# The second mixer as one phase: gates, heads, head norm and output product share one stream of weight tiles, with pairs of heads overlapped

## The reference, cut to what matters

```python
def _mlstm_mix(x, w_in, conv_w, conv_b, b_i, b_f, hn_w, w_out):
    p = x @ w_in                                   # 1024 -> q,k (64 per head), v,o (128 per head), 16 gates
    qk = silu(causal_dwconv(p[..., :1024], conv_w, conv_b))
    v, o, gi, gf = ...                             # the other columns of p
    log_i = softcap(gi + b_i);  log_f = log_sigmoid(softcap(gf + b_f))
    # per head, F = cumsum(log_f), m_t = the running stabiliser:
    # w[t, s]  = exp(F_t - F_s + log_i_s - m_t) * (q_t . k_s) / 8      for s <= t
    # num = w @ v;  den = max(|sum_s w|, exp(-m_t));  h = num / den
    h = h * rsqrt(mean(h * h, -1) + 1e-6) * hn_w   # over the 128 values of a head
    return (h * sigmoid(o)) @ w_out

x = x + g1 * _mlstm_mix(rms(x) * (1 + sc1) + sh1, ...)
```

## Time and profile before

| what | value |
|---|---|
| median of 3 runs | 4840.05 us (4831.29 to 4841.23) |
| the profiled execution | 4829.72 us, span 4828.0 us |
| second mixer, from the end of the norm ahead of it to its last instruction | 3925.0 to 4382.4 us of the span, 457.4 us |
| of that: gates, heads, head norm with the wait for the output weights, output product | 37.3, 313.7, 58.0, 48.4 us |
| TensorE busy in the span | 4274.8 us (89%) |
| mean granted TensorE clock | 0.942 of full speed |

### The profile page before, as it was taken

One profiled execution on the slowest core, in us unless ns is written; L12 is line 12 of the kernel. 1 busy time (PEld: TensorE's weight loads), 2 busy tenths in 40 slices (PEclk: granted clock), 3 DMA queues, 4 the chain that ended last, 5 costly groups with the idle time before them and its releaser, 6 DMA issues. The chain is left out here.

```text
span 4828.0 us, 65725 instructions
## 1 busy us (share of the span) xinstructions
PE 4274.8 (89%) x25274; PEld 3197.5 (66%) x25274; DVE 2312.4 (48%) x4304; ACT 1472.0 (30%) x1985; POOL 1312.9 (27%) x534
## 2 busy tenths in 40 slices
PE   5999879959999999999999779899789868847988
PEld 3777633338888888788888533788668735426866
DVE  6877756547886888322222331556332122353211
ACT  2555510023334444322222101343234111122421
POOL 2322200024443333345454200111234300003432
PEclk9999989989999999999999889899899988868999
DMA  4222177614334555556556221000122211101221
GB/s 148 91 87 93 61 282 285 230 49 131 126 129 159 178 180 178 187 181 195 184 187 190 79 64 51 12 3 3 36 91 96 100 44 52 43 18 65 96 107 53
DMA packets 222607, 548.79 MB, mean 114 GB/s; under 512 B 32272, under 2 KB 100496, under 8 KB 212320
## 3 DMA queue, kind: packets, MB, share of 16 engines
q1 hardware_dynamic: 205472, 546.27, 33.3%
q10 hardware_dynamic: 16960, 0.13, 0.2%
HBM read 470.68 MB, written 75.66 MB: 113 GB/s over the span
## 5 line engine op out<-in xcount | busy, mean ns | idle before, releaser
L1510 POOL TENSOR_TENSOR peer_wl<-peer_wf,peer_wh 128x1024 fp32r<-128x1024 f32 x272 | 717.1, 2637 | 971.1 <-ACT peer_wh L1523 971.1
L1597 PE MATMUL peer_y<-peer_xh,peer_wh 128*128 128x512 f32 x1152 | 455.9, 396 | 30.2 <-DVE peer_xl L1669 30.2
L1523 ACT ACTIVATE peer_wh<-peer_wf 128x1024 fp32r<-128x1024 f32 x272 | 286.2, 1052 | 547.7 <-PE peer_y L1599 513.4
L1599 PE MATMUL peer_y<-peer_xh,peer_wl 128*128 128x512 f32 x1152 | 449.6, 390 | 0.0
L1598 PE MATMUL peer_y<-peer_xl,peer_wh 128*128 128x512 f32 x1152 | 449.5, 390 | 0.0
L1628 PE MATMUL peer_y<-peer_twh,peer_wh 128*128 128x512 f32 x1024 | 405.7, 396 | 11.7 <-DVE peer_twl L1737 11.7
L1629 PE MATMUL peer_y<-peer_twl,peer_wh 128*128 128x512 f32 x1024 | 405.5, 396 | 0.0
L1630 PE MATMUL peer_y<-peer_twh,peer_wl 128*128 128x512 f32 x1024 | 405.5, 396 | 0.0
L1737 DVE TENSOR_TENSOR peer_twl<-peer_gout,peer_twh 128x512 fp32r<-128x512 f32 x128 | 90.8, 710 | 503.6 <-ACT peer_twh L1584 503.6
L1809 PE MATMUL up_acc<-up_xh,up_wh 128*128 128x512 f32 x704 | 276.6, 393 | 47.2 <-DVE up_xl L1859 47.2
L1794 POOL TENSOR_TENSOR up_wl<-up_wf,up_wh 128x1024 fp32r<-128x1024 f32 x88 | 211.3, 2401 | 343.2 <-ACT up_wh L1823 343.2
(11 more groups left out here) (499 smaller groups left out, 8587.4 us busy)
## 6 DMA issues: line engine op xcount, KB each, us to landing
mix_aw<-in_w_ada SPq DMA_DIRECT2D x32, 2048.0 KB, 9.4
peer_wf<-in_u SPq DMA_DIRECT2D x128, 512.0 KB, 3.6
peer_wf<-in_v SPq DMA_DIRECT2D x128, 512.0 KB, 3.7
up_wf<-in_w_gu SPq DMA_DIRECT2D x88, 512.0 KB, 3.2
br_wf<-in_w_in SPq DMA_DIRECT2D x64, 512.0 KB, 3.6
acts<-peer_aout SPq DMA_DIRECT2D x128, 256.0 KB, 2.0
gates<-peer_gout SPq DMA_DIRECT2D x16, 2048.0 KB, 7.3
peer_gout<-gates SPq DMA_DIRECT2D x32, 1024.0 KB, 7.1
```

The costliest lines, as they stand in the source:

```text
L1510: nc.gpsimd.tensor_tensor(wl[:, t % SLOTS], wf[:, t % 2], wh[:, t % SLOTS], ALU.subtract).then_inc(w_low, 1)
L1523: nc.scalar.activation(wh[:, t % SLOTS], wf[:, t % 2], ACT.Copy).then_inc(w_high, 1)
L1597: nc.tensor.matmul(out, wh[:, slot, k], xh[:, k], start=(k == 0), stop=False)
L1599: last = nc.tensor.matmul(out, wl[:, slot, k], xh[:, k], start=False, stop=(k == KT - 1))
```

## The change

One function replaces the four parts. It has one list of 32 weight tiles, 24 for the inputs and 8 for the output, which SP loads, ACT and POOL split and PE consumes in the same order, two buffers deep. All large products are made of three matmuls (lines 2686 to 2688 of the new file, and 2698 to 2700 for the output).

The rounds run i = 0 to 4. In round i PE makes the six products of pair i, and between them the small products of pair i-1 (scores, numerator, denominator, sums of squares), and in front the spread of the normalising factors of pair i-2. The value tiles are now made like the others, and turned by four transposes (`vt`). The denominator is made as a column of sums per token instead of a broadcast matrix: ten matmuls with one column each, whose stationary operand is the weights themselves. Its division and the norm are then done together on tiles of 128x4: DVE's reciprocals (2983, 2994) and ACT's square root (2865). ACT expands the factor to 128x512 (2870), and PE turns it by a product with the identity (2756). The last round has no new products. There PE makes the first six of eight parts of two output tiles (`HELD`) ahead of the last head's norm.

Of the stabilisers only m is stored. The eight broadcast rows are loaded once, into `C.H`, which nobody reads by then. The residual is updated straight from PSUM by one DVE instruction per tile (3060) instead of two.

```diff
-        mlstm_gates_phase(nc, io, C, ngc)
-        mlstm_phase(nc, io, C, h, gate, ngc)
-        norm_phase(nc, C, "mlnorm", h, h, KT, 1, P, EPS_RMS, weight=lambda t: C.v("hn_w", t), times=gate)
-        split_residual_phase(nc, C, "mlout", io["w_ml_out"], KT, 2, 2, 1.0, src=h)
+    mlstm_phase(nc, io, C)
...
             @block.sync
             def _(sp):
+                sp.dma_start(wg[:], io["w_ml_gates"]).then_inc(gates_loaded, 16)
+                for tile, (kind, n) in enumerate(W):
+                    if tile >= 2:
+                        sp.wait_ge(w_low, tile - 1)
+                    sp.dma_start(wf[:, tile % 2], source(kind, n)).then_inc(loaded[tile % 2], 16)
+                    if tile == 3:
+                        sp.wait_ge(rows_ready, 2)
+                        sp.dma_start(io["stabilisers"][0], m).then_inc(m_stored, 16)
+                        sp.wait_ge(m_stored, 16)
+                        for h in range(2 * PAIRS):
+                            sp.dma_start(C.H[:, h], io["stabilisers"][0, h:h + 1].broadcast_to([P, S])
+                                         ).then_inc(rows_loaded, 16)
...
             @block.tensor
...
+                for i in range(PAIRS + 1):
+                    p, cur = i - 1, i < PAIRS
+                    if cur:
+                        project("q", i)
+                    if p >= 0:
+                        scores(2 * p)
+                    if cur:
+                        project("k", i)
+                    if p >= 0:
+                        scores(2 * p + 1)
+                    if p >= 1:
+                        spread(2 * p - 2)
+                        spread(2 * p - 1)
+                    if cur:
+                        project("v", 2 * i)
...
+                    if cur:
+                        project("g", 2 * i)
+                        turn_v(2 * i + 1)
+                    else:
+                        output(0, 0, HELD)
+                        output(1, 0, HELD)
...
             @block.scalar
...
+                def w_highs(tile):
+                    if tile >= len(W):
+                        return
+                    act.wait_ge(loaded[tile % 2], 16 * (tile // 2 + 1))
+                    if tile >= SLOTS:
+                        act.wait_ge(rounds, R.index[W[tile - SLOTS]] + 1)
+                    nc.scalar.activation(wh[:, tile % SLOTS], wf[:, tile % 2], ACT.Copy).then_inc(w_high, 1)
...
+                def keep_numerator(h):
+                    if h >= 2:
+                        act.wait_ge(o_low, h - 1)
+                    keep("n", h, num[:, h % 2])
+                    act.wait_ge(kept_s, R.place["n", h])
+                    nc.scalar.activation(sq[:, h % 2], num[:, h % 2], ACT.Square).then_inc(squared, 1)
...
             @block.vector
...
+                for i in range(PAIRS + 1):
+                    p, cur = i - 1, i < PAIRS
+                    if p >= 0:
+                        weights(2 * p)
+                        weights(2 * p + 1)
+                    if p >= 1:
+                        output(2 * p - 2)
+                        output(2 * p - 1)
+                    if cur:
+                        conv("q", i)
+                        conv("k", i)
+                    if p >= 1:
+                        output_low(2 * p - 2)
+                        output_low(2 * p - 1)
...
+                        decays(2 * i)
+                        decays(2 * i + 1)
+                    if p >= 0:
+                        combine(2 * p)
+                        combine(2 * p + 1)
+                        variance(2 * p)
+                        variance(2 * p + 1)
+                        invert(2 * p)
+                        invert(2 * p + 1)
```

More of the change, by code:

```diff
@@ L2517, in _ @@
                 output(last_pair)
[L2520 to L2533 removed]
+ML_PAIRS = 4
@@ L2545, in _, with result @@
             def _(pe):
[L2546 to L2552 removed]
+                stream = [0]
+                def result(name, n):
+                    pe.wait_ge(kept_s if R.who[name, n] == "s" else kept_v, R.place[name, n])
@@ new lines, in output @@
+                def output(n, first, end):
+                    out = begin("y", n) if first == 0 else of("y", n)
+                    pe.wait_ge(w_low, ML_TILES + n + 1)
+                    s = (ML_TILES + n) % SLOTS
+                    for kk in range(first, end):
+                        pe.wait_ge(o_low, kk + 1)
+                        nc.tensor.matmul(out, wh[:, s, kk], oh[:, kk], start=(kk == 0), stop=False)
+                        nc.tensor.matmul(out, wh[:, s, kk], ol[:, kk], start=False, stop=False)
+                        last = nc.tensor.matmul(out, wl[:, s, kk], oh[:, kk], start=False, stop=(kk == KT - 1))
+                    return last
@@ new lines, in spread @@
+                def spread(h):
+                    pe.wait_ge(f_rows, h + 1)
+                    out = begin("f", h)
+                    for tb in range(TB):
+                        at_b = slice(tb * P, (tb + 1) * P)
+                        last = nc.tensor.matmul(out[:, at_b], frow[:, h % 2, at_b], C.ident[:], start=True, stop=True)
+                    last.then_inc(rounds, 1)
+                pe.wait_ge(gates_loaded, 16)
+                for n, name in enumerate(("gi", "gf")):
+                    product(nc, begin(name, 0)[0:8], wg[:, :, 8 * n:8 * n + 8], C.H, KT).then_inc(rounds, 1)
@@ L2570, in _ @@
+                output_high(2 * LAST)
+                output_high(2 * LAST + 1)
+                for tile in range(ML_TILES + SLOTS, len(W)):
+                    w_highs(tile)
             @block.vector
@@ L2572, in _ @@
                 link = Chain(dve, chain_s)
[L2573 to L2580 removed]
+                tt, ts, stt = nc.vector.tensor_tensor, nc.vector.tensor_scalar, nc.vector.scalar_tensor_tensor
@@ L2752, in second_block @@
+                for h in (2 * LAST, 2 * LAST + 1):
+                    output(h)
+                    output_low(h)
+                for n in range(KT):
+                    x = C.X[:, n]
+                    kept(stt(out=x, in0=read("y", n), scalar=C.mod[:, COL + n:COL + n + 1], in1=x, op0=ALU.mult,
+                             op1=ALU.add), "y", n)
 def second_block(nc, io, C):
```

546 lines of the change are left out of this document (351 added, 195 removed).

## The result

The changed kernel takes 4673.62 us (median of 4 runs, 4669.78 to 4678.82); the kernel before took 4840.64 beside it (4 runs, 4831.29 to 4842.41). The ratio is 0.9659, with a 95% interval from 0.9642 to 0.9677. The forecast was 4678, range 4655 to 4706.

A forecast was written before the change was run, and what follows sets the result against it. The mixer was bound by engine-to-engine chains with barriers, afterwards by PE's own work. Gates, rounds and end made it 156.8 us shorter: 4672.9 from the profiled execution, 4683.3 off the median; forecast the middle, 4678, range 4655 to 4706.

The forecast's parts named there:

- The likeliest case: Whole program: PE's own work bounds the rounds, no stall within one; forecast 4678 us, chance 0.62.
- PE's work: A full round: six products at 5.63 us, denominators 2.3 per head (4.3 at the lower clock), together 52.2.
- The link that I had called the tightest: Next round's first weight tile: ready 49 us after the round's start, wanted by PE at 52.
- The fifth tile: Round 0: tile load waits behind the store of `m` and eight row loads; 6 us charged, bounds 0 and 13.
- DVE beside POOL: Each round: six meetings with POOL passes slow DVE by 1.8 us each, making DVE 34; it still fits.
- the signs that I had named for a right prediction: Mixer near 300 us, PE over 92% busy, rounds about 52, few PE waits at fifth tile and end, longer convolution steps.
- The end: After the fourth round, a chain through ACT, DVE and PE to the last eviction: 83.3 us, bounds 70 and 95.
- The middle between the two sums: Whole program: 4678, between 4672.9 (from the profiled execution) and 4683.3 (off the median of the runs).
- Stalls in every round: Rival: two PE stalls per round in three rounds add 33 us, 4711; one short stall each, 4690; chance 0.22.
- Better than the sum: Rival: row loads hide and the clock recovers sooner in the end, taking off 7.5 and some 8: 4662; chance 0.13.
- The clock at its lower level throughout: Rival: many small matmuls keep PE at its lower level, 216 us lost against 157 gained: 4894; chance 0.01.
- No overlap: Rival: each round is a serial pass, others' 35 us behind PE's 52; three rounds add 105, 4783; chance 0.02.

The follow-up runs named there:

- rows_late: Changed kernel with the store of `m` and the eight row loads issued behind the sixth tile's load instead of the fourth's: 4670.74 us, ratio 0.9649.
- dve_twice: Changed kernel with convolutions and decay weights computed twice on DVE, same result: 4679.98 us, ratio 0.9674.
- two_pass: Changed kernel without the pass of `wh` against `xl` in the 24 input products, 192 matmuls fewer: 4644.72 us, ratio 0.9610.
- tail: rows_late with the last round reordered: sums of squares, three eighths of output tile 0, spreads, then the rest so tile 0 ends first: 4667.31 us, ratio 0.9643.
- tail_wide: tail with 128 columns of ones in place of one in the matmuls of denominators and sums of squares: 4662.98 us, ratio 0.9630.
- four_pass: Changed kernel with a product of the two low halves added to each of 24 input tiles, 192 matmuls more: 4717.31 us, ratio 0.9756.
- ctrl: The changed kernel once more, nothing altered: 4673.45 us, ratio 0.9659.
- products_first: Changed kernel with a round's six products in a row, then all small matmuls of the pair before: 4679.86 us, ratio 0.9668.
- sums_first: Changed kernel with the last sums of squares ahead of the held output product and the spreads between its two tiles: 4670.21 us, ratio 0.9647.
- both: Changed kernel with the edits of rows_late and sums_first together: 4668.48 us, ratio 0.9647.
- plain_f32: Changed kernel with one float32 product of the high halves in place of the three passes of each input product: 4708.32 us, ratio 0.9734.
- two_pass_wide: two_pass with 128 columns of ones in place of one in the denominator matmuls: 4640.08 us, ratio 0.9584.

## Why the prediction was right

The likeliest case came true: PE bound in the rounds, one wait in round 0, a chain in the end. Its terms against the profile, in the order of the sum:

| step | forecast | measured |
|---|---|---|
| gates' load and product | 19.1 | 18.9 |
| round 0 with the fifth tile | 43.3 | 42.3 |
| of which that wait | 6 | 5.4 |
| rounds 1, 2, 3 | 50.4, 52.2, 52.2 | 49.5, 51.2, 51.3 |
| end | 83.3 | 78.6 |
| mixer | 300.5 | 291.8 |

**PE's work.** The products took 5.5 us each and the denominators 2.15 from start to start, against 5.63 and 2.3. I read my prices in `branches_phase` and in the pairs before; these small excesses make the 1 us a round. The choice of 2.3 and not 4.3 for the denominators was right, but my ground (they stand between products) covers only half of what the experiments show: their own price is 2.15 in all the profiles, and it is the product behind them that can run at the lower level.

**Slack.** The link that I had called the tightest, the next round's first tile, came out as told: ready 47.8 after the start of round 2 where I had 49, and wanted at 51.2 where I had 52. (The low half's pass ran from 4092.88 to 4095.28, the product began at 4098.68, the round before at 4047.43.)

**The fifth tile.** The store of `m` came where the sum had put it: forecast 3957.2, in a phase that in this execution began 11.8 later, so 3969.0.

```profile
3969.28 0.35 SPq L2647 DMA_DIRECT2D stabilisers<-ml_e  x1
3970.77 3.67 SPq L2650 DMA_DIRECT2D H<-stabilisers  x8
3974.48 22.23 SPq L2644 DMA_DIRECT2D ml_wf<-in_w_ml  x5
...
3981.23 1.06 ACT L2825 ACTIVATE ml_wh<-ml_wf 128x1024 fp32r<-128x1024 f32 x1 [8.10 <-DMA ml_wf<-in_w_ml]
...
3984.86 0.76 PE L2686 MATMUL ml_bank<-ml_xh,ml_wh 128*128 128x512 f32 x1 [5.37 <-POOL ml_wl L2660]
```

rows_late showed the cause. That the wait came out so near the 6 that I charged has luck in it. The terms that I named (2 for the store, 5 for the eight issues, 3.3 for the load) end at 3967.5, and I wrote 3970 without a term for the rest; in this execution that is 3979.3 and 3981.8. Measured, the store and the issues took less (5.2 from 3969.28 to 3974.48), and the load, beside the eight row loads, took 6.7 where I had 3.3: ACT's high half could start at 3981.23.

**DVE beside POOL.** Here a size was off. I charged 1.8 us for each of six meetings, 34 us of DVE a round; it was 23.5. No convolution step was slowed in the full rounds: eighteen of them, 752 ns each; at most the last of a group was still running when POOL's pass began. In rounds 2 and 3 POOL's passes hold up one group of masks and one of low halves:

```profile
4056.82 2.40 POOL L2660 TENSOR_TENSOR ml_wl<-ml_wf,ml_wh 128x1024 fp32r<-128x1024 f32 x1 [5.97 <-ACT ml_wh L2825]
4057.57 2.39 DVE L2963 TENSOR_TENSOR ml_e<-ml_e,keep 128x128 f32<-128x128 f32 x4
...
4072.65 2.70 POOL L2660 TENSOR_TENSOR ml_wl<-ml_wf,ml_wh 128x1024 fp32r<-128x1024 f32 x1 [7.40 <-ACT ml_wh L2825]
4073.05 3.44 DVE L3006 TENSOR_TENSOR ml_ol<-ml_num,ml_oh 128x512 fp32r<-128x512 f32 x2
```

The masks took 2.39 against 0.90 elsewhere, the low halves 3.44 against 1.47: two meetings, 1.5 and 2.0 lost. The price per meeting was about right and the count wrong. It did not matter, as dve_twice shows. Of the signs that I had named for a right prediction two failed: the convolution steps did not get longer, and the end had five waits of PE where I had named two or three (3.30, 1.43, 1.44, 1.06 and 1.14 us).

**The end.** My chain had the right links in the right order, and each was forecast 6 to 19% late. From the start of the last round ACT's roots were done at 6.4 (I had 7.5), the rows of factors at 7.8 (9.3), DVE's weights at 13.0 (14.6), the sums at 20.5 (22.6), the held part at 28.8 (31), and the third output tile began at 44.3 (47). I had added 3.4 for the clock after the wait; the spreads and the first numerator took 2.6 more than in a full round (3.78 and 3.17 us against 2.05 and 2.32). The 1.5 that I had added for the clock ahead of the last six products was not there: they started at the upper level.

**Where two errors met.** The mixer was 8.7 us better than my sum, and yet the median is only 4.4 below the forecast. The rest of the program, which is the same code, ran longer beside it. This stretch of `branches_phase` in the profile before:

```profile
400.00:605.00 205.00, 186.55 (x959) 144.59 (x958) 165.54 (x298) 110.10 (x188) 51.34 (x21) 0.95 0.23 74
```

and after:

```profile
400.00:605.00 205.00, 192.36 (x966) 151.14 (x968) 154.59 (x269) 103.93 (x172) 52.26 (x22) 0.93 0.23 76
```

The last split product of that part began its last slice at 582.7 us in the profile before, at 597.2 in that of the changed kernel, and between 587.6 and 601.6 in the profiles of the experiments, with no change to its code. The mixer's gain of 165.6 less 13.2 lost elsewhere is the 152.4 by which the spans differ (4828.0 to 4675.6). The profiled execution before lay 10.3 below the median of its runs, so it was a quick one, and this stretch is a likely place for it; but it is the only profile of the kernel before, and all thirteen later ones are behind it here, so that a part of the lag belongs to the changed program is not excluded. The middle between the two sums had no mechanism behind it. Taken off the median alone, my sum gave 4683.3, 9.7 too much, and nearly all of that is the 8.7 of the mixer; that the forecast came within 4.4 owes half to luck.

**The rivals.** Stalls in every round: none. Better than the sum: it named the row loads and the recovery of the clock; the row loads were not hidden (5.4 of wait in place of 6), and the end was indeed 4.7 better. The clock at its lower level throughout: the granted clock of the rounds was 1.00, but its mechanism, many small matmuls, exists and took 1.5 to 3.2 us of a round in two_pass. No overlap: refuted by a round of 51 us.

## What to carry to other kernels

Once independent work fills the waits, price a round by the start-to-start times of PE's instructions alone, and check that the other engines' sums stay below; here an error of 10 us in DVE's sum changed nothing, since DVE had some 27 us of slack in a round. Chains between engines at the beginning and the end of a phase stay visible and are worth following queue by queue, since another order there (another place for a store, an output tile finished earlier) gave some 6 us by the medians (tail), and 10 together with the wider small matmuls (tail_wide), both at the edge of what these runs can tell. Before moving small matmuls together, look at how many one-column ones will stand in a row: the work behind them may pay for it at the lower clock, and giving them 128 columns costs almost nothing.

## What was not expected of the hardware

The granted clock of TensorE fell in the middle of a dense product with no idle time before it, and each time a group of one-column matmuls stood just ahead: the first slow row was one of the group's own or came up to 1.6 us behind its end. It fell behind five of the six denominators of the full rounds in two_pass (0.92 and 0.96 in two of these rounds) and in four_pass (0.95), behind one of six in ctrl (0.97 in round 1), behind the groups of rounds 1 and 2 in products_first (0.93 and 0.97), and in the last round of rows_late, sums_first, both and tail. In plain_f32 the product behind each second denominator took 8.65 us and the one behind each first 6.95, which looks like the same. In the full rounds of the changed kernel, rows_late, sums_first, both, dve_twice and tail, with the same one-column matmuls, it did not fall at all. With 128 columns per matmul it fell neither in the full rounds of two_pass_wide (1.00) nor in the end of tail_wide, where the one-column forms of the same order had it.

So the number of columns is very likely a cause, as two_pass_wide against two_pass and tail_wide against tail show, with one profile each. What else decides in which execution and round the clock falls stays open: four_pass has more dense work between the denominators than the changed kernel and yet lost more.
